# Rounding copies of a norm moved from ScalarE to GpSimd in a two-layer block kernel

## The reference, cut to what matters

```python
for layer in range(2):
    h = rms_norm(x, norm_w[layer, 0]) * (1.0 + sc_m) + sh_m
    y = even_mixer(h, ...) if layer % 2 == 0 else odd_mixer(h, ...)
    x = x + g_m * rms_norm(y, norm_w[layer, 1])
    h = rms_norm(x, norm_w[layer, 2]) * (1.0 + sc_f) + sh_f
    y = conv_ffn(h, ...)
    x = x + g_f * rms_norm(y, norm_w[layer, 3])
```

## Time and profile before

| | |
|---|---|
| Median of 3 runs | 2390.57 us (2389.66 to 2392.43) |
| The profiled execution | 2392.75 us, its span 2391.0 us |
| PE busy | 2336.8 us (98% of the span) |
| DVE busy | 2013.6 us (84%) |
| ACT busy | 1042.1 us (44%) |
| POOL busy | 14.7 us (1%), 22 instructions |
| Mean granted TensorE clock | 0.995 |

### The profile page before, as it was taken

One profiled execution on the slowest core, in us unless ns is written; L12 is line 12 of the kernel. 1 busy time (PEld: TensorE's weight loads), 2 busy tenths in 40 slices (PEclk: granted clock), 3 DMA queues, 4 the chain that ended last, 5 costly groups with the idle time before them and its releaser, 6 DMA issues.

```text
span 2391.0 us, 32706 instructions
## 1 busy us (share of the span) xinstructions
PE 2336.8 (98%) x12476; PEld 2005.7 (84%) x12476; DVE 2013.6 (84%) x2843; ACT 1042.1 (44%) x1159; POOL 14.7 (1%) x22
## 2 busy tenths in 40 slices
PE   8999999999999999999989999999999999999998
PEld 7789897788888888888778888878888888888886
DVE  7779998999989999899888778888888688877875
ACT  2134444544433444344465554635443334433343
POOL 0000010000000000000000000000000000000000
PEclk9999999999999999999999999999999999999999
DMA  9999977677798778977858545475556755576553
GB/s 394 412 392 375 376 259 273 245 256 260 264 371 334 258 268 310 377 264 252 341 193 311 199 170 183 151 298 186 192 184 217 289 207 193 185 275 232 186 193 141
DMA packets 114767, 625.74 MB, mean 262 GB/s; under 512 B 12801, under 2 KB 13249, under 8 KB 63441
## 3 DMA queue, kind: packets, MB, share of 16 engines
q1 hardware_dynamic: 113938, 619.81, 69.8%
q10 hardware_dynamic: 704, 4.23, 0.5%
HBM read 621.85 MB, written 2.13 MB: 261 GB/s over the span
## 4 chain that ended last, share of the span: by engine, by line
PE 81%; DVE 9%; DMA 6%; ACT 3%; issue 1%; DVEq 0%; ACTq 0%
PE bank L2119 32%; PE bank L2121 17%; PE bank L2146 9%; PE bank L2148 9%; PE bank L2147 9%; DMA region<-ada_pieces 4%; DVE lo L1115 3%; DMA piece<-ada_pieces 2%; DVE piece L1138 1%; PE bank L2116 1%; PE bank L2117 1%; DVE region L1138 1%; ACT hi L641 1%; PE bank L2025 1%; PE bank L1882 0%
## 5 line engine op out<-in xcount | busy, mean ns | idle before, releaser
L2119 PE MATMUL bank<-act,hi 128*128 128x512 f32 x3328 | 1048.4, 396 | 5.4 <-DVE act L1200 2.9
L641 ACT ACTIVATE hi<-raw 128x2048 fp32r<-128x2048 f32 x375 | 718.0, 1915 | 766.5 <-PE bank L2148 402.7
L1115 DVE TENSOR_TENSOR lo<-raw,hi 128x2048 fp32r<-128x2048 f32 x375 | 857.6, 2287 | 131.7 <-ACT hi L641 131.3
L2121 PEld LDWEIGHTS bank<-act,lo 128*128 128x128 f32 x3616 | 670.0, 188 | 147.5
L2121 PE MATMUL bank<-act,lo 128*128 128x256 f32 x3616 | 711.9, 278 | 0.0
L2119 PEld LDWEIGHTS bank<-act,hi 128*128 128x128 f32 x3328 | 507.0, 189 | 7.8 <-DVE act L1200 3.3
L2146 PE MATMUL bank<-hi,mid 128*128 128x512 f32 x704 | 274.8, 390 | 3.6 <-DVE lo L1115 3.5
L2147 PE MATMUL bank<-lo,mid 128*128 128x512 f32 x704 | 274.0, 389 | 0.0
L2148 PE MATMUL bank<-hi,mid 128*128 128x512 f32 x704 | 273.9, 389 | 0.0
L1138 DVE SCALAR_TENSOR_TENSOR piece<-piece,cond 128x1024 f32<-128x1024 f32 x206 | 248.7, 1218 | 8.5 <-DMA piece<-ada_pieces 8.5
L2146 PE MATMUL bank<-hi,act 128*128 128x512 f32 x512 | 204.6, 400 | 6.1 <-DVE lo L1115 3.3
(11 more groups left out here) (213 smaller groups left out, 1834.8 us busy)
## 6 DMA issues: line engine op xcount, KB each, us to landing
raw<-w_units SPq DMA_DIRECT2D x378, 1024.0 KB, 4.8
piece<-ada_pieces SPq DMA_DIRECT2D x206, 512.0 KB, 5.6
region<-ada_pieces SPq DMA_DIRECT2D x136, 512.0 KB, 7.6
raw<-head_units SPq DMA_DIRECT2D x16, 1024.0 KB, 16.0
y<-ada_pieces SPq DMA_DIRECT2D x30, 512.0 KB, 6.9
extra<-ada_pieces SPq DMA_DIRECT2D x12, 512.0 KB, 5.8
region<-gamma_scratch ACTq DMA_DIRECT2D x4, 1024.0 KB, 8.2
x<-x_in SPq DMA_DIRECT2D x2, 1024.0 KB, 6.2
```

The costliest lines, as they stand in the source:

```text
L641: sc.activation(hi[:, slot, :], raw[:, raw_slot, :], ACT.Copy).then_inc(s_hi, 1)
L1115: ve.tensor_tensor(lo[:, slot, :], raw[:, raw_slot, :], hi[:, slot, :].bitcast(F32), ALU.subtract).then_inc(s_lo, 1)
L2119: pe.matmul(both, w, act[:, k, :], start=k == 0, stop=False)
L2121: i_ = pe.matmul(dst, w, act[:, k, 0:T], start=False, stop=k == DK - 1)
```

## The change

ScalarE's copy of a pair to the high half of `act` goes away; GpSimd does it in a function of its own, `round_pairs`, ahead of its other work in each phase with a norm, and waits for the scaling of the pair on `s_na`. VectorE takes low part 0 before half update 2 instead of after it. TensorE turns pair 2 not before the products of pair 0 but behind them, just ahead of pair 3.

```diff
@@ ScalarE, pre_norm
-                def high(p):
-
-                    sc.wait_ge(s_na, len(SCALAR_SCALES) * (q - 1) + SCALAR_SCALES.index(p) + 1)
-                    sc.activation(act[:, 2 * p:2 * p + 2, 0:T], normed_pair(p), ACT.Copy).then_inc(s_hh, 1)
-
...
                 for p in SCALAR_SCALES:
                     scaled(p)
-                    high(p)
@@ GpSimd
+            def round_pairs(q):
+
+                for p in SCALAR_SCALES:
+                    gp.wait_ge(s_na, len(SCALAR_SCALES) * (q - 1) + SCALAR_SCALES.index(p) + 1)
+                    gp.tensor_copy(act[:, 2 * p:2 * p + 2, 0:T], normed_pair(p)).then_inc(s_hh, 1)
+
             for ph in PHASES:
+                if ph.norms:
+                    round_pairs(2 * ph.layer + int(ph.kind == "ff_up"))
@@ VectorE, pre_norm
                 normed(0)
-                half_update(2)
                 ve.wait_ge(s_nv, 2 * q)
                 low(0)
+                half_update(2)
                 for p in range(1, 6):
@@ TensorE
                     first_transposes(q)
-                    for p in range(1, 3):
-                        x_transposes(q, p)
+                    x_transposes(q, 1)
...
                         if first_body(i) and j == 0 and ph.norms:
                             q = 2 * ph.layer + int(ph.kind == "ff_up")
+                            if kt == 2:
+                                x_transposes(q, 2)
                             if 2 <= kt <= 10:
                                 x_transposes(q, kt // 2 + 2)
```

## The result

The changed kernel is slower: 2402.22 us median of 5 runs (2401.16 to 2404.4) against 2390.16 of 5 (2389.66 to 2392.43), ratio 1.0049, 95% interval 1.0038 to 1.0060. A second measurement (e12) gave 1.0036 (1.0024 to 1.0049). The forecast was 2401, range 2394 to 2408.

A forecast was written before the change was run, and what follows sets the result against it. TensorE, busy 98%, was taken as the bound. Three norms at 7.1 us (middle of two orders of copies and VectorE operations) plus 3.4 for the clock made 10.5 on 2390.57: 2401 us, range 2394 to 2408.

The forecast's parts named there:

- Exclusion: GpSimd's copies and VectorE's two-input operations shut each other out in the norms; each copy holds the path 0.47 us.
- order B: In the norms, a copy enters behind VectorE's current operation; low parts 1.76 to 1.78 us apart, 5.2 us over three norms.
- order A: In the norms, VectorE's queued operations go ahead of a waiting copy; next low part at 2.00, 9.0 us over three norms.
- Tail: Behind low part 5 of a norm: the last pair's product late by 1.85 (order B) or 3.2 us (order A).
- low part 0 ahead of the update: At a norm's start on VectorE: low part 0 can start at 1643.2 instead of 1643.85, 0.65 us earlier.
- the third pair behind products: At a norm's start, TensorE turns pair 2 0.79 us later; product at 1648.3 against 1648.24, a wash, 0.05 us either way.
- ScalarE relieved, nothing gained: In the norms' pairs: ScalarE loses 7 x 0.63 us per norm, no gain, as TensorE's 1.59 stands right behind.
- The clock: Behind the norms' tails: TensorE's idle of about 2.7 us drops its clock in two of three norms, 3.4 us.
- The copy's own cost: GpSimd's 128x512 copy in the norms takes 0.62 us alone; the skill page's 769 ns would add some 3 us.
- the sum of 10.5: Whole kernel: 7.1 us for three norms plus 3.4 us for TensorE's clock, set on the median.

The follow-up runs named there:

- e12: The changed kernel measured again, unaltered, beside other runs on one chip: 2402.16 us, ratio 1.0036 to the kernel before.
- e3: Kernel before, plus GpSimd copying each scaled pair to a place nobody reads, VectorE waiting once behind low part 7: 2399.49 us, ratio 1.0025.
- e4: Kernel before, plus GpSimd filling 128x512 with zeros per pair, reading nothing, VectorE waiting once behind low part 7: 2390.47 us, ratio 0.9991.
- e2: Kernel before with only the copies moved to GpSimd, at its own order: 2400.64 us, ratio 1.0036.
- e9: Changed kernel with the next weight unit's low part, behind low part 5, as four operations of 512 columns instead of one of 2048: 2403.65 us, ratio 1.0047.
- e5: Changed kernel with the copies of pairs 6 and 7 back on ScalarE: 2397.19 us, ratio 1.0021 to the kernel before.
- e1: Changed kernel with the copies of pairs 1 to 7 back on ScalarE, both order edits kept: 2394.99 us, ratio 1.0007 to the kernel before.
- e8: Kernel before with only low part 0 moved ahead of half update 2: 2397.05 us, ratio 1.0019.
- e7: Changed kernel with nine unused 128x128 matmuls on TensorE in the idle time ahead of pair 6: 2401.86 us, ratio 1.0039 to the kernel before.

## Why the prediction was right, point by point

- **Exclusion.** Right in kind, and shown by e3 against e4. The copies cost 1.89 x 3 = 5.7 us (e2), order B's walk gave 5.2 for all the edits and the middle of A and B, which went into the sum, 7.1. The pace was order B's (1.75 where B had 1.76 to 1.78). That B's 1.85 per norm is so near 1.89 is partly luck: it had low part 5 1.24 us late and the tail another 0.6, measured in e2 0.94 and 0.95.
- **Order.** Neither A nor B throughout. In the pairs the copy got in behind the operation that VectorE was in; in the tail it asked 0.06 us behind the start of the unit's low part and waited it out, where B had let it in ahead. One rule covers both, and e9: who asks first holds the path for one operation. That is also what the Trainium skill says (SBUF — State Buffer, section SBUF: two separate sides), and the trace agrees: 1658.14 (in between two updates) and 1659.88 (behind 2.28 us). The row at 303.68, where a queued operation of VectorE went ahead of a waiting copy, isn't explained by it and stays open.
- **Tail.** The last pair's product was forecast 1.85 (B) or 3.2 us (A) late. The products of pair 6 and of pair 7 both came 2.63 us late with all edits, of which e5 gives 0.96 to the tail's copies.
- **The order edits: the step that failed.** I priced low part 0 ahead of the update as 0.65 us earlier, and the third pair behind products as "a wash, 0.05 us either way". Low part 0 did start 0.59 earlier (2.72 us behind the first turning in e1, 3.31 in e4), but nothing came of it: the update that pair 2 needs now stands behind it. The two edits together cost 0.77 us per norm (e1), 2.3 in all, and low part 0 first alone costs 0.82 (e8); the second edit on top of it is the wash. My comparison went wrong in two ways. I followed pair 2 to its product (1648.3 against 1648.24) and not to its low part, which leads to low part 5 and the norm's end. By my own numbers low part 2 was to start at 1644.75 + 2.8 = 1647.55, and before it started half a microsecond earlier:
```profile
1647.05 0.69 DVE L1200 TENSOR_TENSOR act<-region,act 128x512 fp32r<-128x512 f32 x1 [0.20 <-ACT act L692]
```
And the row was of a norm in which TensorE had just run at half rate and was late itself. At full clock pair 2 is turned 3.45 us behind the first, with both order edits 4.34, in the changed kernel 4.61 (1646.43 to 1651.04), and ScalarE and VectorE behind it have no time to spare to make that good.
- **ScalarE relieved, nothing gained.** As forecast: e2 has ScalarE's 7 copies less and is slower by 1.89 us per norm.
- **The clock: 3.4 us forecast, not shown as a cause.** Two of three tails were followed by half rate, as forecast, and apart from the end of the span the trace had seven lengths of 3.4 us at half rate (the one at the second norm's beginning counts twice) against five before, worth 2 x 1.7. But before, the norms' beginnings had three of them; e7 took away those behind the tails and was no faster. The measured difference is 12.1 us in the first comparison (2402.22 less 2390.16), of which the norms are 7.9. The remaining 4.2 are of the size of the clock's coming and going and aren't settled further; the second measurement, 0.36% or 8.6 us, leaves only 0.7 of it.
- **The copy's own cost.** Rounding is recorded as another operation (CAST) than the copies before, and took 0.62 us where it ran free, as assumed. The 769 ns for 512 elements that the Trainium skill gives (GPSIMD Engine Reference, section Performance versus the Vector engine) don't hold for it here.

So the sum of 10.5 was near the measured 12.1 partly by luck. For the norms it had 7.1 against 7.9: order B, whose pace it was, gave 5.2 alone; the order edits, priced as a wash, cost 2.3; and averaging with order A, which only the tail's first copy followed, put 1.9 in their stead. For the clock it had 3.4, and what is left to it is 4.2 in one measurement and 0.7 in the other.

## What to carry to other kernels

A copy that GpSimd makes beside a busy VectorE is paid in VectorE's time when its operations have two inputs in SBUF: count into VectorE's step what the copy keeps it waiting (0.36 us of the copy's 0.62 here, 1.23 less 0.87) and ask whether that step then becomes the pace. Where two edits move work within a pipeline of several engines, follow the item that comes later than before through every engine to the end of the stage, and take the times to compare with from a stretch at full clock; one at half rate hides lateness on every other engine.

## What the runs showed of the hardware that I had not expected

Fills by GpSimd (0.52 us for 128x512) ran beside VectorE's two-input operations with neither being longer, copies of the same size, which read there too, stretched an update from 0.48 to 0.90 us. And the half-rate stretches move with small changes of the schedule: apart from the end of the span the profiled executions had between three (e4) and nine (e3, e12) lengths of 3.4 us at half rate. At 1.7 us each the six between them are worth up to 10 us, an estimate, so that a difference of 2 us in such a kernel is better read from a norm at full clock than from the whole time.
